# First stage of a four-stage layer pair: the modulation's sums as TensorE products of the loaded pieces

## The reference, cut to what matters

```python
def adaln_params(c, w, b):
    mod = jax.nn.silu(c) @ w + b
    shift, scale, gate = jnp.split(mod, 3, axis=-1)
...
h = rms_norm(x, norm_g[i]) * (1.0 + scale) + shift
...
proj = h @ w_in            # queries, keys, values (and the gates, in the second stage)
```

## Time and profile before

| | us |
|---|---|
| median of three runs | 1536.61 |
| lowest and highest | 1533.77, 1537.57 |
| the profiled execution | 1540.15 |
| its span, first to last instruction | 1538.4 |
| TensorE busy in the span | 1435.4 (93%) |
| VectorE, ScalarE, GpSimd busy | 890.7, 538.0, 386.1 |

### The profile page before, as it was taken

How to read it: one execution, slowest core, us unless ns; L and a number is a source line. 1 busy time by engine, 2 the same in 40 slices (tenths; PEclk the granted TensorE clock), 3 DMA queues, 4 the chain that set the end, 5 groups by cost and what they waited for, 6 DMA issues and landing times.

```text
span 1538.4 us, 20207 instructions
## 1 busy us (share of the span) xinstructions
PE 1435.4 (93%) x7240; PEld 1210.9 (79%) x7240; DVE 890.7 (58%) x1524; ACT 538.0 (35%) x1270; POOL 386.1 (25%) x551
## 2 busy tenths in 40 slices
PE   1789999999899997789999999899999999999999
PEld 1577777788678786778888888688888888888887
DVE  7766677665434446787777775535456452645522
ACT  2433344333301115775556564322222222222200
POOL 2333333312222222454555555320000000000000
PEclk9999999999989998999999999999999999999999
DMA  8644555534987686766767765941111552112142
GB/s 309 212 165 160 197 191 191 193 121 160 345 309 275 261 321 220 268 245 232 263 251 277 274 240 194 334 126 41 55 42 62 171 193 74 42 55 75 49 150 82
DMA packets 96787, 285.62 MB, mean 186 GB/s; under 512 B 10768, under 2 KB 40496, under 8 KB 87088
## 3 DMA queue, kind: packets, MB, share of 16 engines
q1 hardware_dynamic: 87760, 250.74, 45.3%
q0 software_dynamic: 8928, 33.59, 6.2%
HBM read 196.22 MB, written 88.08 MB: 185 GB/s over the span
## 4 chain that ended last, share of the span: by engine, by line
PE 68%; DMA 9%; DVE 9%; issue 5%; ACT 4%; POOL 3%; SPq 1%; ACTq 0%; DVEq 0%; POOLq 0%
PE po_f_ps L1843 23%; PE po_y_ps L1859 11%; PE at_y_ps L1415 9%; PE qk_proj L667 7%; PE ga_g_ps L933 6%; PE at_o_ps L1399 5%; PE at_s_ps L1371 3%; DMA ga_ada<-in_ada_w 3%; DMA values_split<-qk_late 2%; PE at_tr L1381 2%; DMA po_xn<-x_mid_t 1%; POOL qk_rq L306 1%; ACT at_pr L1191 1%; POOL qk_acc L297 1%; DMA ga_raw<-in_attn_w_gate 1%
## 5 line engine op out<-in xcount | busy, mean ns | idle before, releaser
L1843 PE MATMUL po_f_ps<-po_ht,po_w 128*128 128x512 f32 x1536 | 348.9, 389 | 0.0
L1843 PEld LDWEIGHTS po_f_ps<-po_ht,po_w 128*128 128x128 f32 x1536 | 288.1, 188 | 60.1 <-DVE po_ht L1705 0.3
L667 PE MATMUL qk_proj<-qk_w_qkv,qk_ht 128*128 128x512 f32 x1152 | 281.9, 401 | 14.2 <-DVE qk_ht L460 8.2
L667 PEld LDWEIGHTS qk_proj<-qk_w_qkv,qk_ht 128*128 128x128 f32 x1152 | 216.9, 192 | 60.9 <-DVE qk_ht L460 9.3
L1415 PE MATMUL at_y_ps<-at_zt,at_w 128*128 128x512 f32 x768 | 197.0, 398 | 6.2 <-DVE at_x L1304 6.2
L1859 PE MATMUL po_y_ps<-po_zt,po_w 128*128 128x512 f32 x768 | 174.7, 389 | 0.0
L1859 PEld LDWEIGHTS po_y_ps<-po_zt,po_w 128*128 128x128 f32 x768 | 144.1, 188 | 29.9
L1415 PEld LDWEIGHTS at_y_ps<-at_zt,at_w 128*128 128x128 f32 x768 | 137.3, 189 | 31.4 <-issue 7.4
L1692 DVE TENSOR_TENSOR po_w<-po_raw,po_w 128x1024 fp32r<-128x1024 f32 x48 | 58.8, 1225 | 129.2 <-ACT po_w L1626 129.2
L1147 POOL TENSOR_SCALAR_AFFINE_SELECT at_pt<-at_ph 128x512 fp32r<-128x512 f32 x128 | 83.6, 676 | 187.6 <-ACT at_ph L1198 187.6
L306 POOL TENSOR_TENSOR qk_rq<-qk_mq,qk_half 128x8 f32<-128x8 f32 (+1 forms) x48 | 71.2, 1484 | 189.1 <-DVE qk_mq L487 189.1
(11 more groups left out here) (168 smaller groups left out, 2013.0 us busy)
## 6 DMA issues: line engine op xcount, KB each, us to landing
at_w<-out_weight_split SPq DMA_DIRECT2D x32, 1024.0 KB, 6.3
queries_t<-qk_late SPq DMA_DIRECT2D x16, 1024.0 KB, 4.2
ga_ada<-in_ada_w POOLq DMA_DIRECT2D x64, 256.0 KB, 4.5
at_qt<-queries_t SPq DMA_DIRECT2D x16, 1024.0 KB, 8.1
ht_split<-qk_ht SPq DMA_DIRECT2D x6, 2048.0 KB, 9.6
values_split<-qk_late SPq DMA_DIRECT2D x16, 768.0 KB, 4.9
at_vs<-values_split SPq DMA_DIRECT2D x16, 768.0 KB, 4.9
qk_late<-in_ada_w SPq DMA_DIRECT2D x16, 512.0 KB, 6.1
```

Source lines behind the costliest of these rows:

```text
L667: last = nc.tensor.matmul(proj[:, b * BANK:(b + 1) * BANK], ht[:, s % 2, m, k, t * P:(t + 1) * P], w_qkv[:, w, k, b * BANK:(b + 1) * BANK] ...
L1843: last = nc.tensor.matmul(f_ps[:, bank(j, h), :], w[:, i % 2, a, k, :], ht[:, h, m, k, :], start=(n == 0), stop=(n == 3 * KC - 1))
```

## The change

The weighted adds on VectorE and `sums` go. TensorE multiplies each piece as it lands: 8 products, each with a 128x128 block of the piece as weights and the column of silu(c) that belongs to its rows moving, into a PSUM column of its own (64 for shift, 64 for scale). VectorE reduces the 64 columns to 8, then bias and scale follow. The slots are 7 instead of 5, so 7 items of w_qkv borrow them, and only items 10 and 11 return to `raw`. Items 0, 1 and 2 are requested behind pieces 9, 11 and 13. The four small loads go to GpSimd's queue. The additions of x's squares go from GpSimd to VectorE, where both angle reductions now come first; ScalarE makes its squares behind Sin and Cos. TensorE sums the squares behind piece 11 and spreads the root behind piece 14. The memset of `vs` waits for the eighth split. In the third stage `wg_hi` and `wg_lo` are merged with `fold_hi` and `fold_lo`, each wait counting the same instructions as before (shown in part).

```diff
@@ -131,7 +131,7 @@
     BANK_HEADS = [(0, HEADS // 2), (HEADS // 2, HEADS), (HEADS, QK)]
-    AS, MODC, SPAN = 5, 2 * KC, D
+    AS, MODC, SPAN = 7, 2 * KC, D
     ADA = 2 * D // SPAN * KC
@@ -164,7 +164,6 @@
     ada = late[:, 0:AS * SPAN].rearrange("p (a n) -> p a n", a=AS)
-    sums = late[:, AS * SPAN:AS * SPAN + 2 * D]
     qs = late[:, 0:2 * D].rearrange("p (h d) -> p h d", h=HEADS)
@@ -182,7 +181,7 @@
     trig_arg, pre_done = sem("trig_arg"), sem("pre_done")
-    ada_added, mod_summed = sem("ada_added"), sem("mod_summed")
+    ada_added = sem("ada_added")
     sqx_done, acc_done, st_done, mx_done, rx_done = (sem(n) for n in ("sqx_done", "acc_done", "st_done", "mx_done", "rx_done"))
@@ -197,6 +196,8 @@
     BORROWED = range(RAW, RAW + AS)
+    EARLY_W = {9: 0, 11: 1, 13: 2}
+    FIRST_W = 2 * KC // KP
 
@@ -210,7 +211,6 @@
 
-    MOD_PARTS = ((0, KC), (KC, KC + KC // 2), (KC + KC // 2, MODC))
     THIRDS = ((0, 1, 2), (3, 4, 5), (6, 7))
@@ -262,11 +262,9 @@
                 load_x(0)
-                sp.dma_start(bias[:, :], ada_b[0]).then_inc(small_loaded, 16)
-                sp.dma_start(g_col[:, :], norm_g[0]).then_inc(small_loaded, 16)
-                sp.dma_start(gq[:, :], q_norm[0].partition_broadcast(P)).then_inc(small_loaded, 16)
-                sp.dma_start(gk[:, :], k_norm[0].partition_broadcast(P)).then_inc(small_loaded, 16)
-        for i in range(ITEMS):
+            if i in EARLY_W:
+                load_w(EARLY_W[i])
+        for i in range(RAW, ITEMS):
             load_w(i)
@@ -305,9 +303,12 @@
 
-        add_squares(0, range(KC))
+        pool.dma_start(bias[:, :], ada_b[0]).then_inc(small_loaded, 16)
+        pool.dma_start(g_col[:, :], norm_g[0]).then_inc(small_loaded, 16)
+        pool.dma_start(gq[:, :], q_norm[0].partition_broadcast(P)).then_inc(small_loaded, 16)
+        pool.dma_start(gk[:, :], k_norm[0].partition_broadcast(P)).then_inc(small_loaded, 16)
         rstd_x(0)
-        pool.wait_ge(mod_summed, len(MOD_PARTS))
+        pool.wait_ge(w_lo, FIRST_W)
         nc.gpsimd.memset(vs, 0.0).then_inc(consts_set, 1)
@@ -381,18 +382,18 @@
         nc.scalar.activation(c_tanh[:, :], c_col[:, :], ACT.Tanh, scale=0.5).then_inc(act_begun, 1)
-        square_x(0, range(KC))
         act.wait_ge(trig_arg, 1)
...
         nc.scalar.activation(cos[:, :, 0:HALF], red2, ACT.Sin).then_inc(act_begun, 1)
+        square_x(0, range(KC))
         for i in range(RAW):
...
                 w_high(RAW)
-        for i in range(RAW + 1, RAW + AS):
+        for i in range(RAW + 1, FIRST_W):
             w_high(i)
@@ -468,14 +469,11 @@
 
-        def add_ada(i):
-            k, part = i % KC, sums[:, i // KC * SPAN:(i // KC + 1) * SPAN]
-            dve.wait_ge(ada_loaded[i % AS], 16 * (i // AS + 1))
-            if k == 0:
-                nc.vector.tensor_scalar(part, ada[:, i % AS, :], c_silu[:, 0:1], None, ALU.mult).then_inc(ada_added, 1)
-            else:
-                dve.wait_ge(ada_added, i)
-                nc.vector.scalar_tensor_tensor(part, ada[:, i % AS, :], c_silu[:, k:k + 1], part, ALU.mult, ALU.add).then_inc(ada_added, 1)
+        def add_first_squares():
+            for k in range(1, KC):
+                dve.wait_ge(sqx_done, k + 1)
+                wait(dve, acc_done, k - 1)
+                nc.vector.tensor_tensor(acc[:, :], acc[:, :], sqx[:, k % SQ], ALU.add).then_inc(acc_done, 1)
 
@@ -540,14 +538,16 @@
 
-        def set_scale(part):
-            cols = slice(*MOD_PARTS[part])
-            dve.wait_ge(mod_summed, part + 1)
-            nc.vector.tensor_tensor(mod[:, cols], tr[:, part, 0:KC // 2], bias[:, cols], ALU.add).then_inc(pre_done, 1)
-            dve.wait_ge(pre_done, 2 * part)
-            nc.vector.scalar_tensor_tensor(mod[:, cols], mod[:, cols], 1.0, g_col[:, (part - 1) * KC // 2:part * KC // 2],
-                                           ALU.add, ALU.mult).then_inc(pre_done, 1)
+        def set_mod(part):
+            cols = slice(part * KC, (part + 1) * KC)
+            dve.wait_ge(ada_added, KC * (part + 1))
+            nc.vector.tensor_reduce(mod[:, cols], tr[:, part, 0:KC * KC].rearrange("p (j k) -> p j k", k=KC), AX.X, ALU.add).then_inc(pre_done, 1)
             dve.wait_ge(pre_done, 2 * part + 1)
+            nc.vector.tensor_tensor(mod[:, cols], mod[:, cols], bias[:, cols], ALU.add).then_inc(pre_done, 1)
+            dve.wait_ge(pre_done, 2 * part + 2)
+            if part == 1:
+                nc.vector.scalar_tensor_tensor(mod[:, cols], mod[:, cols], 1.0, g_col[:, :], ALU.add, ALU.mult).then_inc(pre_done, 1)
+                dve.wait_ge(pre_done, 5)
 
@@ -569,25 +569,20 @@
             link(nc.vector.tensor_scalar(ang[:, :, f], pos_f[:, :], float(inv_freq[f]), None, ALU.mult))
-        for i in range(ADA):
-            add_ada(i)
-            if i == 4:
-                reduce_angle(0.0, red)
-            if i == 9:
-                reduce_angle(0.25, red2)
-            if i == ADA - 7:
-                mean_x(0)
-        for i in range(RAW):
+        reduce_angle(0.0, red)
+        reduce_angle(0.25, red2)
+        add_first_squares()
+        mean_x(0)
+        w_low(0)
+        dve.wait_ge(small_loaded, 64)
+        set_mod(0)
+        for i in range(1, RAW):
             w_low(i)
-        dve.wait_ge(small_loaded, 64)
-        dve.wait_ge(mod_summed, 1)
-        nc.vector.tensor_tensor(mod[:, 0:KC], tr[:, 0, 0:KC], bias[:, 0:KC], ALU.add).then_inc(pre_done, 1)
-        set_scale(1)
+        set_mod(1)
         modulate(0, range(KC // 2))
-        set_scale(2)
         w_low(RAW)
         modulate(0, range(KC // 2, KC))
-        for i in range(RAW + 1, RAW + AS):
+        for i in range(RAW + 1, FIRST_W):
             w_low(i)
@@ -692,13 +687,17 @@
         pe.wait_ge(consts_set, 4)
-        for part, (first, end) in enumerate(MOD_PARTS):
-            pe.wait_ge(ada_added, KC if part == 0 else ADA)
-            for j in range(first, end):
-                last = nc.tensor.matmul(tr[:, part, j - first:j - first + 1], sums[:, j * P:(j + 1) * P], ones[:, :], start=True, stop=True)
-            last.then_inc(mod_summed, 1)
-            if part == 0:
+        pe.wait_ge(silu_done, 2)
+        for i in range(ADA):
+            part, k = i // KC, i % KC
+            pe.wait_ge(ada_loaded[i % AS], 16 * (i // AS + 1))
+            for j in range(KC):
+                last = nc.tensor.matmul(tr[:, part, j * KC + k:j * KC + k + 1], ada[:, i % AS, j * P:(j + 1) * P], c_silu[:, k:k + 1],
+                                        start=True, stop=True)
+            last.then_inc(ada_added, 1)
+            if i == ADA - 5:
                 sum_squares(pe, 0)
+            if i == ADA - 2:
                 spread(pe, 0)
@@ -1015,8 +1014,13 @@
     fold_loaded, wg_loaded, fold_stored = ring("fold_loaded", 3), ring("wg_loaded", 2), ring("fold_stored", 2)
-    fold_hi, fold_lo, wg_hi, wg_lo, fold_done, fold_out = (sem(n) for n in (
-        "fold_hi", "fold_lo", "wg_hi", "wg_lo", "fold_done", "fold_out"))
+    fold_hi, fold_lo, fold_done, fold_out = (sem(n) for n in ("fold_hi", "fold_lo", "fold_done", "fold_out"))
+
+    def wg_split(f):
+        return f * (PAIRS + 1) + 1
+
+    def wv_split(u):
+        return wg_split(u // PAIRS) + u % PAIRS + 1
 
@@ -1062,9 +1066,11 @@
         if pair == 0:
-            wait(sp, wg_lo, f - 1)
+            if f >= 2:
+                sp.wait_ge(fold_lo, wg_split(f - 2))
             sp.dma_start(wg_raw[:, f % 2], w_group[GC * f:GC * (f + 1)].rearrange("c p n -> p c n")).then_inc(wg_loaded[f % 2], 16)
-        wait(sp, fold_lo, u - 2)
+        if u >= 3:
+            sp.wait_ge(fold_lo, wv_split(u - 3))
         sp.dma_start(wv_raw[:, u % 3], wvt[GC * f:GC * (f + 1)][:, :, pair * ROWS:(pair + 1) * ROWS].rearrange("c p n -> p c n")).then_inc(fold_loaded[u % 3], 16)
```

More of the change, by code:

```diff
@@ L1223, in fold_high @@
                 wait(act, fold_done, PAIRS * (f - 1))
-                nc.scalar.activation(wg[:, f % 2, HI], wg_raw[:, f % 2], ACT.Copy).then_inc(wg_hi, 1)
+                nc.scalar.activation(wg[:, f % 2, HI], wg_raw[:, f % 2], ACT.Copy).then_inc(fold_hi, 1)
             act.wait_ge(fold_loaded[u % 3], 16 * (u // 3 + 1))
@@ L1309, in fold_low @@
             if u % PAIRS == 0:
-                dve.wait_ge(wg_hi, f + 1)
-                nc.vector.tensor_tensor(wg[:, f % 2, LO], wg_raw[:, f % 2], wg[:, f % 2, HI].bitcast(F32), ALU.subtract).then_inc(wg_lo, 1)
-            dve.wait_ge(fold_hi, u + 1)
+                dve.wait_ge(fold_hi, wg_split(f))
+                nc.vector.tensor_tensor(wg[:, f % 2, LO], wg_raw[:, f % 2], wg[:, f % 2, HI].bitcast(F32), ALU.subtract).then_inc(fold_lo, 1)
+            dve.wait_ge(fold_hi, wv_split(u))
             nc.vector.tensor_tensor(wv[:, u % 3, LO], wv_raw[:, u % 3], wv[:, u % 3, HI].bitcast(F32),
@@ L1423, in fold @@
             if h == 0:
-                pe.wait_ge(wg_lo, f + 1)
-                pe.wait_ge(fold_lo, u + 1)
+                pe.wait_ge(fold_lo, wv_split(u))
                 wait(pe, fold_out, u - 1)
```

## The result

The changed kernel took 1566.81 us, median of 4 runs (1563.7 to 1567.86), against 1537.09 us for the kernel before, measured beside it (4 runs, 1533.77 to 1545.7). The ratio is 1.0186, with a 95% interval of 1.0163 to 1.021: slower by 1.9%. The profiled execution took 1563.7 us for a span of 1561.9 us, 23.5 us more than the profiled one of the kernel before.

The account below looks back on a forecast made before the run. TensorE's products bound the span, and TensorE's 16 modulation pieces at 1.2 GHz become the first stage's bound; projection starts at 66.7 instead of 43.19, all else nothing: 1536.6 + 23.5 = 1560 us, range 1555 to 1567.

Parts of the forecast that it names:

- The 4.42 us turn: Modulation before the change: gap-free one-column products from 23.36 to 27.78 us, taken as evidence the clock stays at 1.2 GHz.
- rival A: Modulation stream: clock rises after two pieces, later pieces cost 1.58 us, projection starts at 38.2, time 1531.6 us; chance 0.08.
- The price of a piece: Modulation stream: eight one-column products on TensorE at 1.2 GHz cost 3.55 us, bounds 3.49 to 3.6, for 16 pieces.
- the spread: TensorE's spread of rstd behind piece 15 of the modulation, four instructions: 0.87 us.
- the way from the last product to the projection: End of modulation: semaphore 0.1, VectorE's reduction, bias and scale 0.7, then 1.6 to the first projection.
- +23.5: Predicted delay in us of the first projection, from 43.19 to 66.7, carried whole into the kernel's time.
- The memset: GpSimd's memset of 1.38 us, moved behind the eighth split in the first tile: hidden, at most 0.4 us if uncovered.
- the sign named for a wrong forecast: First tile: a third bank starting later behind the first than the 18.7 us of the kernel before.
- B: Modulation stream: clock rises late or now and then, half the pieces at each price, +7.3 us, 1544; chance 0.05.
- C: First tile: item 9, x, items 10 and 11 queue on SyncE, up to 10 us late, 1566 to 1570; chance 0.06.
- D: First tile: TensorE's 3.54 us wait for splits is saved by making them during the stream, 1556; chance 0.03.
- item 11: First tile: this weight item comes earlier, which could save at most ScalarE's 0.43 us wait; taken as 0.

Follow-up runs that it names:

- before_again: The kernel before, unaltered, run once more for a second trace: 1537.09 us in one execution.
- after_again: The changed kernel, unaltered, run on another occasion: 1565.58 us, ratio 1.0181 to the kernel before.
- loads_alone: The kernel before with only the change's loads: small ones on GpSimd's queue, three w_qkv items among the modulation's pieces; 1538.36 us, ratio 1.0002.
- warm_first: The changed kernel with five unused products of 512 columns ahead of the modulation's stream: 1564.14 us in one execution.
- fold_alone: The kernel before with only the third stage's merged fold semaphores: 1538.65 us, ratio 0.9999.
- wide32: The changed kernel with 32 equal columns moving in each modulation product instead of one: 1565.76 us in one execution.
- pe_pad: The kernel before with 200 small unused bfloat16 products in TensorE's idle start: 1544.63 us, ratio 1.0036.
- memset_cover: The changed kernel with vs in other slots, so its memset waits for the sixth split, not the eighth: 1566.76 us in one execution.
- pe_pad256: The kernel before with 256 small unused products in TensorE's idle start: 1538.58 us, ratio 1.001.
- wide128: The changed kernel with 128 equal columns moving in each modulation product instead of one: 1541.22 us, ratio 1.0012 to the kernel before.
- hybrid1: The changed kernel with VectorE adding the scale half and TensorE multiplying the shift half, one column moving, six slots: 1547.59 us in one execution.
- hybrid128: The changed kernel with VectorE adding the scale half and TensorE multiplying the shift half, 128 columns moving, six slots: 1540.99 us, ratio 1.002.

## Why the prediction was right, and where not

The marks of the stage by trace (us; start of the first projection, from there to the second tile, gate stage):

```
before        43.2  28.2  205.0      after         64.3  29.3  206.0
before_again  41.3  28.6  202.0      after_again   64.5  29.3  206.9
loads_alone   42.6  27.6  204.3      warm_first    62.7  28.1  208.9
fold_alone    40.9  28.7  203.5      wide32        64.5  28.1  209.1
pe_pad        43.3  28.2  210.1      memset_cover  64.4  28.1  209.4
pe_pad256     41.6  28.3  206.6      wide128       40.7  29.3  206.9
hybrid1       45.2  28.7  207.4      hybrid128     41.7  28.1  208.0
```

- **The mechanism** was right: TensorE carries the stage alone, at 1.2 GHz, from the first piece to the last. The clock was read off durations, against a column that says 1.00 without a record; wide128 shows the same 1.00 in 5:9, where a piece takes 3.54 us, and half the time after 10. The 4.42 us turn, on which the refusal of rival A rested, was the right witness; in warm_first the same kind of products ran without a pause for longer, and the clock fell under them.
- **The price of a piece** was mis-sized: 3.55 us predicted, 54.55 / 16 = 3.41 measured. 3.55 is a turn that stands alone, with its beginning and end; in a stream these overlap (hybrid128's lone last piece takes 3.56 again). Sixteen times 0.14 are 2.2 us, and 3.41 lies below the bound of 3.49. The first piece began 0.17 sooner, the spread took 1.06 in place of 0.87, and the way from the last product to the projection 2.28 in place of 2.4: together the start at 64.33 in place of 66.7, +21.1 in place of +23.5.
- **The memset** was costed at nothing, "uncovered it would be 0.4 at most". That looked at who waits for GpSimd, and not at what VectorE does beside it: it cost 1.1 us by way of VectorE (the changed kernel's 29.3 us from first projection to second tile against 28.1 in memset_cover), and the sign named for a wrong forecast, a third bank more than 18.7 us behind the first, came true (19.8; 18.6 in memset_cover).
- **The base.** The +23.5 between the two profiled executions is the sum to the tenth, but by luck: +21.1 at the start, +1.1 from the memset, and 1.3 from differences behind it, of which 1.0 is the gate stage. The trace of before also had the latest start of its kind; over the four traces that have that kernel's modulation and no added products it is 42.0, which makes the shift 22.4.
- **Behind the stage** nothing was expected. The gate stage was 206.0 and 206.9 us in the two traces of the changed kernel against 203.7 on average over those four: +2.8. pe_pad shows that such a difference can come with added instructions that cost no time of their own; that it is so in the changed kernel is likely and not shown.
- **What remains.** The mean span of the two traces of the changed kernel is 1562.6, that of the four traces 1538.1: 24.5 us. The ratios make 28 to 29 us of 1537. Both profiled executions of the changed kernel were the quickest of their four; the gate stages of 208.9 to 209.4 in its three near copies would bring 2 to 3 us more. That the unprofiled runs have these is likely and not shown. The median, 1566.8, is thus 7 above the forecast and inside the range of 1555 to 1567 by 0.2 us. That it is inside is a narrow thing: the price of a piece was put 2.2 us too high in sum, and costs that the prediction had at nothing made up for that and more.
- **The rivals.** A (the clock rises in the stream, 1531.6) failed for this kernel by its own row. The rule of the Trainium skill behind it, page "TensorE: Matmul & The Clock Gate", section "What's actually happening", that sustained activity releases the clock, held here for 128-column products (from 9.8 us in wide128) and for 512-column ones, not for 1 and 32 columns, however steadily TensorE worked. Its time was too good as well: with the clock up, wide128 starts at 40.7 and not at 38.2, as pieces cost 1.8 to 2.1 us and not 1.58, and arrive late once. With one column at the higher clock a piece cost 1.7 to 1.8 us in warm_first, so the 1.58, a turn of 0.79 us doubled, was too low in itself. B, a part at each level, did not occur. C (covers fail, up to 10 us) did not: no transfer is late in the first tile. D, a part comes back, did not: the wait for splits ahead of the third bank was 4.71 us and, without the memset's share, 3.53, against 3.54 before.
- **Loads, fold semaphores, squares, item 11**: costed at nothing, and nothing that can be told in loads_alone and fold_alone; the squares' adds were done at 23.6, 23 us ahead of their use. Item 11 was in no run by itself.

## What to carry to other kernels

Work moved from a busy engine to an idle one must be priced at the state the idle engine is in: here TensorE's one-column products cost 3.41 us a piece at 1.2 GHz, against VectorE's 1.3 us, while a piece arrives every 1.3 us; made wide, at no other cost, they came near enough to be neutral. Ask of each moved instruction which engine works beside it in its new place, not only who waits for it. And a difference of a third of a per cent behind an edit that lengthens an instruction list may come with the list itself: fill the list in idle time, to another length, and look whether the difference goes.

## What the runs showed of the hardware

- One-column float32 products with a 128x128 weight load each kept TensorE occupied for 56.5 us, and every piece cost what it costs at 1.2 GHz (3.41 us); in warm_first the clock fell from 2.4 to 1.2 GHz under them without a pause in the work (1.7 to 1.8 us a piece, then 3.41). At the lower clock a piece cost the same with 1 and with 32 columns: 41.09 and 41.14 us for twelve. With 128 columns the clock was up by the second piece.
- A memset of GpSimd (128x1536) and small float32 operations of VectorE wait for each other, and with starts 10 ns apart in the records either can be the one that waits: 1.49 us in place of 0.22 for VectorE, or 1.64 in place of 1.40 for GpSimd.
- 200 products in idle time at the beginning made the kernel slower by 0.36%, through the gate stage, which begins at 376 us; 256 cost 0.1% at a 95% interval from -0.02% to 0.21%.
